# One encoder layer on one core: the last head pair, the routing and the first and last expert slots put in another order

## The reference, cut to what matters

```python
mod = silu(c) @ ada_w + ada_b                       # shift, scale, gate of both halves
h = rmsnorm(x) * (1 + sc1) + sh1
q, k, v = split(h @ sb_w_qkv)                       # 16 heads of 64
x = x + g1 * (stick_breaking(q, k, v, cache) @ sb_w_o)
h = rmsnorm(x) * (1 + sc2) + sh2
s = sigmoid(h @ router_w)                           # 16 experts in 4 groups
# per token: best group by the sum of its two best (s + bias), two best experts in it,
# gates = s of the two / their sum
out = sum(gate_e * ((silu(h @ w_gate[e]) * (h @ w_up[e])) @ w_down[e]) for e in chosen)
y = rmsnorm(x + g2 * out)
```

## Time and profile before

| | |
|---|---|
| runs | 883.05, 880.73, 882.36 us |
| the profiled execution | 882.33 us, of which the span is 880.6 |
| TensorE busy | 774.8 us (88%), mean granted clock 0.949 |
| VectorE, ScalarE, GpSimd busy | 591.2 (67%), 470.1 (53%), 87.1 us (10%) |
| moved by DMA | 214.86 MB, mean 244 GB/s |
| chain that ended last | PE 77%, DVE 8%, DMA 7%, issue 3%, POOL 2%, ACT 2% |

### The profile page before, as it was taken

One profiled execution on the slowest core, in us unless ns is written; L12 is line 12 of the kernel. 1 busy time (PEld: TensorE's weight loads), 2 busy tenths in 40 slices (PEclk: granted clock), 3 DMA queues, 4 the chain that ended last, 5 costly groups with the idle time before them and its releaser, 6 DMA issues.

```text
span 880.6 us, 13491 instructions
## 1 busy us (share of the span) xinstructions
PE 774.8 (88%) x4168; PEld 588.0 (67%) x4169; DVE 591.2 (67%) x742; ACT 470.1 (53%) x527; POOL 87.1 (10%) x143
## 2 busy tenths in 40 slices
PE   2899999999999997579980489999999999999776
PEld 0477777878777785358860367777787777877432
DVE  1366574655647463663677668888788887888397
ACT  5225464545546353651313157777777776877503
POOL 2000211112021111120003100000000000000260
PEclk9899999999999999589995589999999999999989
DMA  8928395684949564510007994858799999997642
GB/s 317 348 78 269 80 308 158 229 239 148 342 115 317 145 242 153 188 28 0 1 16 293 360 405 179 329 231 336 300 399 398 386 403 389 395 394 317 229 178 119
DMA packets 95096, 214.86 MB, mean 244 GB/s; under 512 B 4634, under 2 KB 55898, under 8 KB 88931
## 3 DMA queue, kind: packets, MB, share of 16 engines
q1 hardware_dynamic: 89748, 195.21, 61.1%
q0 software_dynamic: 2880, 10.49, 3.2%
q10 hardware_dynamic: 2448, 8.91, 2.5%
HBM read 186.81 MB, written 44.56 MB: 263 GB/s over the span
## 4 chain that ended last, share of the span: by engine, by line
PE 77%; DVE 8%; DMA 7%; issue 3%; POOL 2%; ACT 2%; SPq 1%; DVEq 0%; ACTq 0%; POOLq 0%
PE z L1036 42%; PE fill_ps L1742 17%; PE z L1742 10%; DMA ada_w<-in_ada_w 3%; PE fill_ps L1659 2%; PE z L1137 2%; SPq L1282 1%; PE fill_ps L1665 1%; POOL slots_in L542 1%; PE fill_ps L1166 1%; DMA slots_out<-y_slot 1%; DMA exp_w<-slots_out,fetch_i 1%; PE fill_ps L1036 1%; DVE ew_sp L1588 1%; DMA w_pair<-in_sb_w_qkv 1%
## 5 line engine op out<-in xcount | busy, mean ns | idle before, releaser
L509 DVE TENSOR_TENSOR w_lo<-exp_w,w_hi 128x1024 fp32r<-128x1024 f32 x192 | 223.5, 1220 | 56.3 <-ACT w_hi L505 56.1
L505 ACT ACTIVATE w_hi<-exp_w 128x1024 fp32r (+1 forms) x192 | 196.1, 1055 | 75.1 <-PE z L1036 53.9
L1036 PE MATMUL z<-w_hi,x_slotT_hi 128*128 128x512 f32 x288 | 125.2, 435 | 13.8 <-DVE w_lo L509 11.2
L1036 PE MATMUL z<-w_hi,x_slotT_lo 128*128 128x512 f32 x288 | 116.4, 404 | 0.0
L1036 PE MATMUL z<-w_lo,x_slotT_hi 128*128 128x512 f32 x288 | 116.3, 404 | 0.0
L1742 PE MATMUL fill_ps<-h_hi,wp_hi 128*128 128x512 f32 x192 | 78.1, 407 | 1.4 <-DVE h_lo L1513 1.4
L1742 PE MATMUL fill_ps<-h_lo,wp_hi 128*128 128x512 f32 x192 | 77.1, 401 | 0.0
L1036 PEld LDWEIGHTS z<-w_hi,x_slotT_hi 128*128 128x128 f32 x288 | 55.9, 194 | 30.7 <-DVE w_lo L509 12.2
L1742 PE MATMUL fill_ps<-h_hi,wp_lo 128*128 128x512 f32 x192 | 76.3, 397 | 0.0
L1036 PEld LDWEIGHTS z<-w_lo,x_slotT_hi 128*128 128x128 f32 x288 | 55.9, 194 | 15.8 <-issue 3.8
L1036 PEld LDWEIGHTS z<-w_hi,x_slotT_lo 128*128 128x128 f32 x288 | 55.8, 194 | 13.7
(11 more groups left out here) (321 smaller groups left out, 1458.3 us busy)
## 6 DMA issues: line engine op xcount, KB each, us to landing
exp_w<-in_exp_w_gate SPq DMA_DIRECT2D x19, 2048.0 KB
exp_w<-in_exp_w_up SPq DMA_DIRECT2D x19, 2048.0 KB
exp_w<-in_exp_w_down SPq DMA_DIRECT2D x18, 2048.0 KB
ada_w<-in_ada_w SPq DMA_DIRECT2D x12, 2048.0 KB, 9.4
slots_in<-zeros SPq DMA_DIRECT2D x7, 2048.0 KB, 12.8
w_pair<-in_sb_w_qkv SPq DMA_DIRECT2D x24, 512.0 KB, 5.2
x_slot<-slots_in SPq DMA_DIRECT2D x18, 512.0 KB, 9.1
slots_out<-y_slot ACTq DMA_DIRECT2D x17, 512.0 KB
```

The lines of the kernel that those rows point to most:

```text
L505: act.activation(w_hi[:, u % RING, :].unsqueeze(1), raw_unit(b, u), ACT.Copy).then_inc(hi_ready, 1)
L509: dve.tensor_tensor(w_lo[:, u % RING, :].unsqueeze(1), raw_unit(b, u), w_hi[:, u % RING, :].bitcast(F32).unsqueeze(1), ALU.subtract).then_ ...
L1036: return pe.matmul(out, lhsT, rhs, start=start, stop=stop, skip_group_check=True)
```

## The change

1. *Last pair.* The slice of pair 6 (`modulate`, `keep_slice`) moves from behind that pair into the last pair, ahead of the last slice. `w_o` is loaded before the last slice, not behind it. The six finished o parts are split ahead of the last pair's exp, and w_o's hi parts ahead of its second exp. Output product q=0 for k < 6 stands between `keep_sums` and `values`; q=1 for k < 6 stands between the spreads; both go to `fill_ps`, and k = 6, 7 follow. `pair_ps` changes its banks.
2. *Routing.* Copies of the turned h2 and of `gate2` move from VectorE to ScalarE. The last tile's square is taken in two halves and its scale, shift, turn and copy in halves. Spread 7 stands behind the last `sum_route`. Some routing steps are joined or moved behind the row numbers.
3. *Slot 0.* Its turned rows come from 40 plain fp32 products of `h2_tok` with one-hot matrices `first_pick`, not from the scattered table. VectorE makes slot 0's first four lo units and x_lo ahead of the gates and last picks. The last picks are turned within slot 0's up product; slot 1's gate units start before its rows are turned. The load of expert 1's gate weights is issued ahead of the scatter's end; slot 1's rows are loaded first after it.
4. *End.* The last down load is issued after the third early gather, not ahead of the gathers. All late gate passes come ahead of the last slot's y; late adds 3 and 4 move to GpSimd.

```diff
+        sp.wait_ge(exp_loaded[0], 16)
+        load_expert(sp, 0, 1, 1, None)
         sp.wait_ge(scattered, 16 * 2 * NT)
-        sp.dma_start(x_slot[:, :], slots_in[0:P, :]).then_inc(x_slot_loaded, 16)
+        sp.wait_ge(x_slotT_mm, 1)
         sp.dma_start(y_slot[:, :], slots_in[P:2 * P, :]).then_inc(second_loaded, 16)
+        sp.wait_ge(exp_loaded[1], 16)
+        load_expert(sp, 1, 1, 1, None)
         load_expert(sp, 2, 0, 0, None)
-        for i in range(2):
-            sp.wait_ge(exp_loaded[i], 16)
-            load_expert(sp, i, 1, 1, None)
-        sp.wait_ge(x_slotT_mm, 1)
         sp.dma_start(x_slot[:, :], slots_in[2 * P:3 * P, :]).then_inc(x_slot_loaded, 16)
         sp.wait_ge(exp_loaded[2], 16)
         load_expert(sp, 2, 1, 1, None)
...
+        with sp.Fori(1, m) as j:
...
+        before = next_of(m, -1)
+        sp.wait_ge(down_ready, m)
...
+        sp.wait_ge(early_gathered[TILES[2]], 16)
+        sp.wait_ge(exp_loaded[2], 16 * (m + 1))
+        sp.nop(nofuse=True)
+        load_expert(sp, 2, before[0], before[0] % 2, before[1])
...
+        for t in TILES:
+            sp.wait_ge(gathered[t], 16)
         sp.dma_start(g_fin, io["final_norm_g"].unsqueeze(0).to_broadcast([P, D])).then_inc(rows_loaded, 16)
...
+        for i in range(3, NT):
+            t = TILES[i]
+            pool.wait_ge(late_step, i + 1)
+            pool.wait_ge(x_added[i], 1)
+            pool.tensor_tensor(x_tok[:, t, :], x_tok[:, t, :], late_y[:, t, :], ALU.add).then_inc(all_but_last[i], 1)
...
+        act.wait_ge(proj_added, NT)
+        act.activation(sq_tmp[:, 0:D // 2], x_tok[:, last, 0:D // 2], ACT.Square,
+                       accum_out=std2[:, last:NT]).then_inc(sq_ready, 1)
+        act.wait_ge(sq_ready, NT + 1)
+        squares_of(0)
+        squares_of(1)
+        keep_h2T(0)
+        squares_of(2)
+        keep_h2T(1)
+        squares_of(3)
+        keep_logits(0)
...
+        keep_logits(1)
+        keep_logits(2)
+        act.wait_ge(proj_added, 2 * NT)
+        act.activation(sq_tmp[:, D // 2:D], x_tok[:, last, D // 2:D], ACT.Square,
+                       accum_out=std2[:, last:NT]).then_inc(sq_ready, 1)
+        act.wait_ge(sq_ready, 2 * NT + 1)
...
+        act.wait_ge(std2_ready, NT)
         act.activation(zero_a[:, :], eps1[:, :], ACT.Exp).then_inc(table_set, 1)
+        keep_h2T(3)
+        for i in range(2):
+            if i:
+                keep_logits(3)
+            act.wait_ge(h2T_mm, NT + i)
+            act.activation(h_T[:, 4 * i:4 * i + 4, last * P:NT * P],
+                           turned_h2(last)[:, 512 * i:512 * i + 512].rearrange("p (k c) -> p k c", c=P),
+                           ACT.Copy).then_inc(h2T_kept, 1)
+        keep_logits(last)
...
+        for r in (6, 7):
+            act.wait_ge(rows_mm, r + 1)
+            act.activation(gate2[:, r - 6, :], pair_ps(r), ACT.Copy).then_inc(rows_kept_act, 1)
...
+        this_up(0)
         act.wait_ge(pick_turned, 1)
-        act.activation(last_pick_T[:, :], z[:, 2048:2048 + NT * P], ACT.Copy).then_inc(pick_kept, 1)
-        this_up(0)
+        act.activation(last_pick_T[:, :], z[:, 1024:1024 + NT * P], ACT.Copy).then_inc(pick_kept, 1)
+        next_gate(0, range(RING - 1))
         next_x_hi(0)
-        next_gate(0)
+        next_gate(0, range(RING - 1, RING))
...
+        add_projected(dve, NT)
+        dve.wait_ge(sq_ready, NT + 1)
+        step(dve.tensor_scalar(rstd[:, NT - 1:NT], std2[:, NT - 1:NT], 1.0 / D, EPS, ALU.mult, ALU.add))
+        for t in range(1, NT - 1):
+            add_projected(dve, NT + t)
+            normed(t - 1, 1)
+        normed(NT - 2, 1)
+        add_projected(dve, 2 * NT - 1)
+        normed(NT - 1, 2)
+        dve.wait_ge(consts_b, 12)
...
+        step(dve.tensor_scalar(r_tmp[:, :, :], in_top[:, :, :], -8192.0, 8192.0, ALU.mult, ALU.add))
         step(dve.tensor_tensor(s_e[:, :, :], s_e[:, :, :], in_top[:, :, :], ALU.mult))
...
         dve.wait_ge(places_mm, 1)
...
+        step(dve.tensor_scalar(count[:, :], n_slots[:, :], 1.0, float(P), ALU.max, ALU.mult))
+        step(dve.tensor_tensor_scan(base[:, :], ones_e[:, :], count[:, :], 0.0, ALU.mult, ALU.add))
+        step(dve.tensor_tensor(base[:, :], base[:, :], count[:, :], ALU.subtract))
...
-        step(dve.tensor_scalar(r_tmp[:, :, :], in_top[:, :, :], -8192.0, 8192.0, ALU.mult, ALU.add))
         step(dve.tensor_tensor(sel[:, :, :], rows[:, :, :], r_tmp[:, :, :], ALU.add))
         step(dve.tensor_reduce(row_f[:, :, 0], sel[:, :, :], AX_X, ALU.min))
         dve.tensor_copy(row_i[:, :, :], row_f[:, :, :]).then_inc(rows_known, 1)
+
+        for t in range(NT):
+            dve.tensor_scalar(first_pick[:, t, :], lane_f[:, :], sel[:, t, 0:1], None, ALU.is_equal).then_inc(first_ready, 1)
+        step(dve.tensor_scalar(n_slots[:, :], n_slots[:, :], 1.0, None, ALU.max))
+        step(dve.tensor_tensor_scan(slot_end[:, :], ones_e[:, :], n_slots[:, :], 0.0, ALU.mult, ALU.add))
         step(dve.memset(fetch_w[:, 0:1], 16.0))
 
...
+        step(dve.tensor_reduce(tok1[:, :], s_e[:, :, :], AX_X, ALU.add))
+        step(dve.reciprocal(tok1[:, :], tok1[:, :]))
+        step(dve.tensor_tensor(s_e[:, :, :], s_e[:, :, :], tok1[:, :].unsqueeze(2).to_broadcast([P, NT, NE]), ALU.mult))
+        for u in range(RING):
+            dve.wait_ge(hi_ready, u + 1)
+            lo_unit(dve, 0, u)
+        dve.wait_ge(x_hi_ready, 1)
+        dve.tensor_tensor(x_slotT_lo[:, :, :], z[:, 2048:3072].rearrange("p (k c) -> p k c", c=P),
+                          x_slotT_hi[:, :, :].bitcast(F32), ALU.subtract).then_inc(x_slotT_kept, 1)
         for r, src in ((0, sel), (1, rows)):
...
-        keep_rows(dve, (6, 7))
-        for u in range(RING):
-            dve.wait_ge(hi_ready, u + 1)
-            lo_unit(dve, 0, u)
         dve.wait_ge(scattered, 16 * 2 * NT)
         dve.tensor_copy(zero_f[:, :], eps1[:, :]).then_inc(hid_ready, 1)
-        keep_slotT(0)
...
         rest_of_up(0)
         gate_by_sig(0)
+        rest_of_gate(1, range(RING - 1))
+        keep_slotT(1)
+        rest_of_gate(1, range(RING - 1, RING))
         keep_hid(0)
-        keep_slotT(1)
-        rest_of_gate(1)
...
         keep_hidT(m)
         rest_of_up(m + 1, range(1))
         for i in range(2):
             gated_y(early_y, TILES[i], 0, early_step)
-        rest_of_up(m + 1, range(1, 2))
+        rest_of_up(m + 1, range(1, 3))
         gated_y(early_y, TILES[2], 0, early_step)
-        rest_of_up(m + 1, range(2, RING))
+        rest_of_up(m + 1, range(3, RING))
...
-        for i in range(2):
+        for i in range(NT):
             gated_y(late_y, TILES[i], 1, late_step)
+        for i in range(3):
             add_late(i)
-        dve.wait_ge(x_slot_loaded, 16 * (m + 2))
...
                               ALU.mult).then_inc(last_y_kept, 1)
-        gated_y(late_y, TILES[2], 1, late_step)
-        add_late(2)
...
+        dve.wait_ge(rows_loaded, 64)
+        for i in range(NT):
             finish(i)
...
         pe.wait_ge(ada_kept, 4 + NPAIR)
         pe.wait_ge(bias_loaded, 16)
+        pe.wait_ge(sel_ready, 1)
+        spread(0)
+        spread(1)
+        project_out(pe, 1, range(NPAIR - 2))
         pe.wait_ge(o_kept, 1 + NPAIR)
-        pe.wait_ge(sel_ready, 1)
-        for r in range(6):
-
-            if r == 4:
-                pe.wait_ge(rows_kept_act, 1)
-            elif r >= 3:
-                pe.wait_ge(rows_kept, r // 2)
-            spread(r)
-
-        def project_out(q):
-
-            c, t = divmod(q, NT)
-            if q == 0:
-                pe.wait_ge(rows_kept, 3)
-                pe.wait_ge(rows_kept_act, 2)
-                pe.wait_ge(o_lo_ready, NPAIR)
-            elif q >= 4:
-                pe.wait_ge(proj_kept, q - 3)
-            toks = slice(t * P, (t + 1) * P)
-            for k in range(NPAIR):
-                if t == 0:
-                    pe.wait_ge(wo_lo_ready, c * NPAIR + k + 1)
-                acc(zb(q % 4), o_hi[:, k, toks], wo_hi[:, k, :], start=(k == 0))
-                acc(zb(q % 4), o_hi[:, k, toks], wo_lo[:, k, 512 * c:512 * c + 512])
-                mm = acc(zb(q % 4), o_lo[:, k, toks], wo_hi[:, k, :], stop=(k == NPAIR - 1))
-                if q == NT - 1 and k < NPAIR - 1:
-                    mm.then_inc(wo_used, 1)
-            mm.then_inc(proj_ready, 1)
-
-        def turn_h2(u):
-            pe.wait_ge(h2_ready, u + 1)
-            if u:
+        spread(2)
+        pe.wait_ge(rows_kept, 1)
+        spread(3)
+        project_out(pe, 0, range(NPAIR - 2, NPAIR))
+        project_out(pe, 1, range(NPAIR - 2, NPAIR))
+        pe.wait_ge(rows_kept_act, 1)
+        spread(4)
+        pe.wait_ge(rows_kept, 2)
+        spread(5)
+
...
+        for q in range(2, NT + 3):
+            project_out(pe, q)
+        turn_h2(0)
+        project_out(pe, NT + 3)
+        turn_h2(1)
+        route(0)
+        project_out(pe, NT + 4, range(4))
+        turn_h2(2)
+        sum_route(0)
+        route(1)
+        project_out(pe, NT + 4, range(4, NPAIR))
```

(113 more changed lines are left out.)

183 lines of the change are left out of this document (83 added, 100 removed).

## The result

The changed kernel took 870.45 us (median of 866.42, 869.98, 870.92 and 1978.53) beside 882.7 of the kernel before on the same chip: ratio 0.9847, 95% interval 0.982 to 0.9875, some 13.5 us faster. The ratios leave out two disturbed runs, this one of 1978.53 us and one of 925.58 in the experiment "y early". The forecast was 854 with a range of 844 to 868: the sign is right, half of the gain is missing, and the time lies outside the range. The profiled execution took 869.98 us, its span 868.2 (before 882.33 and 880.6), so the profile shows a gain of 12.35.

The account below looks back on a forecast made before the run. TensorE's products were taken to fill the slot loop, the winnable time lying before and after it. Gains of 25.0 us up to the loop and 3.7 behind it, 28.7 off 882.3, gave 854 us, range 844 to 868.

Parts of the forecast that it names:

- Steps 1 to 3: Last pair and first output products, routing logits, routing steps: gains of 10.9, 6.0 and 0.6 us.
- Step 1: Last pair and first output products, up to the start of product q=2: gain 10.9 us (7 to 13).
- Step 2: Tail of output products and routing logits, up to VectorE's first routing step: 6.0 us more (4.5 to 7.5).
- Step 4: Slot 0, up to its first products: 40 plain fp32 products take 10.8 us; 11.7 us more gain (8 to 15).
- The clock: Rival: TensorE stays at half clock through picks and slot 0's first half; 862 us, chance 0.07.
- Step 5: Between slot 0 and slot 1: hidden waits come out, total gain falls from 29.2 to 25.0 us (20 to 29).
- Step 6: The loop over slots: unchanged, 0 us gain, slot turns of 18.5 us as before.
- loads behind the scatter: Rival, after slot 0: scatter and weight loads share queues worse than the ceiling, TensorE waits; 865 us, chance 0.13.
- loads binding the loop: Rival, slower: weight and row loads, not TensorE, bound the loop's turns; 888 us, chance 0.05.
- Step 7: Behind the loop, gathers ahead of the last weights, up to the last slot's y: gain 3.7 us (-1 to 7).
- the mechanism as a rival: Tail: GpSimd's two late adds and VectorE's three block each other, 3.3 us lost; 857 us, chance 0.11.
- The gathers' own gain: Behind the loop: gathers ahead of the last down load start the last products some 8 us earlier, at 841.3.

Follow-up runs that it names:

- y early: Changed kernel with only the last slot's y moved up behind the second of five late passes; ratio 0.9792 to the kernel before.
- contiguous weights: Changed kernel with slot 0's 40 one-hot products reading contiguous blocks of 128 channels (that slot's output wrong); ratio 0.9793 to the kernel before.
- the repaired tail: Changed kernel, no GpSimd adds behind late gathers, y behind two late passes, sample tile's step behind three adds; 858.02 us, ratio 0.9707.
- gathers behind the weights: Changed kernel with the last down load no longer waiting for the third early gather; ratio 0.9849 to the kernel before.
- slot 0 by rows: Changed kernel picking slot 0's rows by 10 products of 128x512, then turning them; VectorE's scatter wait moved later; ratio 0.9725 to the kernel before.

## Why the prediction was wrong, and where it was right

*Steps 1 to 3* were right: the slice landed at 359.48 (forecast 359.2), and the products that fill the gap ahead of the values cost nothing. Step 1 gave 1.9 us more than I took: the sums behind the slice ran at half clock only at first (0.93 from 364 to 368 us), so the products behind them started at 368.56 and not at 370.6. Step 2's terms come to 6.3, not to the 6.0 that I wrote; it measured 5.9.

*Step 4 failed, in its size.* I wrote: "The same form stands in the sums: from start to start two take 0.37 us at the higher clock, 0.71 at the lower, so 40 take 7.4 to 14.2." The sums' stationary operand is contiguous; these products read every eighth channel. They took 19.32 us, at one pace at both clocks, outside both bounds, and with contiguous weights 12.10, near the 10.8 forecast; slot 0's first products then came at 470.56, where I had 470.6. The clock, which I had made the range and a rival of, cost these products nothing.

The trace of before held a hint, no more: weight loads by line, of turns of a slot's rows (step of 32 bytes), of the hidden rows (16 bytes) and of h2 (contiguous), and the pace of the first:

```profile
L1137 PEld LDWEIGHTS z<-ident,x_slot 128*128 128x128 f32 x136 | 17.4, 197 | 7.2 <-DMA x_slot<-slots_in 7.2
...
L1166 PEld LDWEIGHTS fill_ps<-ident,hid 128*128 128x128 f32 x72 | 11.5, 206 | 3.0 <-DVE hid L932 1.3 <-issue 0.5
...
L1090 PEld LDWEIGHTS z<-ident,h_tok 128*128 128x128 f32 x40 | 4.7, 143 | 3.8 <-issue 3.4
```

```profile
527.10 1.06 PE L1137 MATMUL z<-ident,x_slot 128*128 128x128 f32 x8
527.91 0.48 PE L1036 MATMUL z<-w_hi,x_slotT_hi 128*128 128x512 f32 x1
```

54 ns on each of 80 loads would have given a bound some 4 us higher, and a doubt about the form. But eight such turns take 0.81 us, 0.10 each: no row of before had both the form and the step of the new products, and the step alone slowed nothing there. "SBUF — State Buffer", section "Door 1: The DMA port swizzle (why `[64,N]` ≈ `[32,N]`)", in the Trainium skill, says that each access which crosses into another 16-byte line of SBUF pays, and that 4 fp32 elements is how far one can step for free. 335 ns against 243 agrees with the first, the step here being 8 elements; the 206 ns of the hidden rows' turns, in steps of 4, against 143 do not agree with the second.

*Step 5 came out by luck*, -4.1 for -4.2. I had TensorE idle some 6 us behind slot 0's first half, for the second half's w_lo, which VectorE makes behind its gates and last picks and the scatter's end. In the changed kernel slot 0 came so late that the scatter was over (slot 1's row load went out at 478.85), and TensorE idled 1.83 us, for the 8 us from the gates to the w_lo:

```profile
477.16 0.23 DVE L928 TENSOR_TENSOR r_tmp<-sel,row_f 128x80 f32<-128x80 f32 x1
...
485.20 4.62 DVE L522 TENSOR_TENSOR w_lo<-exp_w,w_hi 128x1024 fp32r<-128x1024 f32 x4
```

What the shorter wait saved went elsewhere: the 24 products of slot 0's first half took 7.3 us and those of the second slot's 7.52, at a granted clock of 0.57 from 477 to 481 us and of 0.55 from 500 to 505, where I had some 5.5 for either; and the wait ahead of the second slot was 5.53 for 4.4. With contiguous weights, where slot 0 came as forecast, the wait was 5.04 us and the step took 6.3. *Step 6* was right: 18.5 us a turn. Of the rivals, loads behind the scatter fell with the scatter's end at some 479 (forecast 480 to 481), and loads binding the loop didn't bind even when slot 1 started 6.8 us sooner still.

*Step 7 failed, in its size and in what it was paid for.* "VectorE now does five gated passes and three adds ahead of the last y, 6.4 + 3.7": they took 10.25 and 7.77. The times in that step leave 5.0 us for the adds (849.5 to 854.5), not its 3.7; against these the passes were 3.9 us over and the adds 2.8, and some 1.3 is a later start: the 7.9 that y lost on the forecast. I had the mechanism as a rival, but priced it for the late adds alone, at 3.3; GpSimd's early adds, which I left out, fall on the passes. The adds' part is an outcome of this profile: in three others the same adds took 3.48, which would have left y some 3.6 us short. Behind y 1.9 us more went, since TensorE had waited 12.02 us and ran its next products at half clock. TensorE's rows before, then after:

```profile
859.62 1.12 PE L1036 MATMUL z<-y_slot,last_pick_T 128*128 128x512 f32 x2 [0.98 <-ACT y_slot L698]
860.58 1.88 PE L1036 MATMUL z<-x_slot,last_pick_T 128*128 128x512 f32 x4
```

```profile
845.33 2.07 PE L1140 MATMUL z<-y_slot,last_pick_T 128*128 128x512 f32 x2 [12.02 <-ACT y_slot L765]
847.20 2.91 PE L1140 MATMUL z<-x_slot,last_pick_T 128*128 128x512 f32 x4
```

The gathers' own gain was forecast well (last products some 8 us sooner; 6.8 measured beside the loop's gain). Undone alone it showed no cost beyond the noise, undone in the repaired tail it cost 5.8 us.

## To carry to other kernels

Price a new product by a row that has both its form and the steps in which its stationary operand is read; where no row has both, widen the range or run the product both ways. Here, at full clock, a step of 32 bytes halved the rate of plain fp32 products, while turns with the same step kept theirs. When work moves to a second engine beside VectorE, list all of its two-input instructions in that stretch, not just those of the same kind, and put what TensorE waits for ahead of them. An undo that costs nothing beyond the noise may only be hidden by what stands behind it: undo it again once that is gone, and compare the stages, not only the ends. A step that comes out right to a tenth can still be right by luck: check the wait that it names.

## What was not expected of the hardware

- In plain fp32 products of 128 columns, loads of 128x128 weights in steps of 32 bytes came every 0.2 us at a granted clock of 0.50 and at 1.00 alike; contiguous ones every 0.17 and 0.10 us. Turns with weights in the same steps came every 0.10 us at 1.00.
- Which engine gets ahead in the tail doesn't follow from which began first: GpSimd's late adds begin 1.04 us before VectorE's in five profiles (the changed kernel, contiguous weights, y early, gathers behind the weights, slot 0 by rows), yet VectorE's took 7.77 or 7.78 us and GpSimd's 6.60 in two, 3.48 and 9.04 in the three others.
- An instruction of 512 columns in plain fp32 took 0.33 us at full clock and 0.67 at half clock.
